# Expert outputs of a mixture of experts put on their tokens by matmuls, in place of scatters to memory and loads

## The reference

```python
def hier_moe(h, ...):
    g_prob = softmax(h @ w_rg + b_rg);  p_top, g_top = top_k(g_prob, 1)
    e_in_group = (h @ w_re + b_re).reshape(n, 4, 8)[arange(n), g_top[:, 0]]
    v_top, i_top = top_k(e_in_group, 2)
    gates = softmax(v_top) * p_top                # two experts of 32 for each token
    ...                                           # tokens sorted by expert, in blocks
    out = (silu(xb @ w_gate[e]) * (xb @ w_up[e])) @ w_down[e]     # each block xb
    y = segment_sum(out * w_buf[:, None], tok_buf)                # gated, summed on the tokens
# after it: x = x + y, then the final RMSNorm
```

## Time and profile before

| | |
|---|---|
| median of 3 runs | 1119.4 us (1118.56 to 1120.49) |
| profiled execution, its own time | 1122.52 us |
| its span | 1120.7 us |
| mean granted clock of TensorE | 0.962 |
| DMA busy share from about 625 us on | 1.0, at about 427 GB/s |

### The profile page before, as it was taken

The page is one execution under the profiler, slowest core; times in us unless marked ns, Lnnn a source line. Parts: engine busy times, 40 slices in busy tenths (PEclk is TensorE's granted clock), DMA queues, the critical chain, the costliest instruction groups (busy, mean ns, idle before and its releaser), DMA issues.

```text
span 1120.7 us, 15303 instructions
## 1 busy us (share of the span) xinstructions
PE 1025.1 (91%) x6339; PEld 701.9 (63%) x6339; DVE 380.1 (34%) x727; ACT 281.6 (25%) x454; POOL 223.6 (20%) x129
## 2 busy tenths in 40 slices
PE   8999999999999999999999899977888889877886
PEld 6996777779999879999998333333333333333332
DVE  7246332233587491421344322111011111111117
ACT  5435434346446442222213100000000000000003
POOL 0331112112312256434330011110011110110000
PEclk9999999999999989999999999999888999998898
DMA  9332411212211213253285999999999999999993
GB/s 225 81 88 79 164 50 39 57 39 74 60 48 39 67 57 91 80 164 100 80 351 224 346 427 426 426 425 427 427 427 427 427 428 427 428 427 425 426 410 136
DMA packets 108943, 267.57 MB, mean 239 GB/s; under 512 B 21821, under 2 KB 88797, under 8 KB 95666
## 3 DMA queue, kind: packets, MB, share of 16 engines
q1 hardware_dynamic: 104178, 258.06, 60.0%
q0 software_dynamic: 4704, 8.64, 2.0%
HBM read 256.12 MB, written 18.17 MB: 245 GB/s over the span
## 4 chain that ended last, share of the span: by engine, by line
PE 37%; DMA 24%; DVE 4%; issue 2%; ACT 2%; POOL 1%; SPq 0%; DVEq 0%; ACTq 0%; POOLq 0%
DMA we<-in_w_exp_up 24%; PE proj L1051 16%; PE proj L1533 12%; PE proj L1549 3%; DVE ors L2089 1%; PE bank L1425 1%; DVE xsT L2536 1%; PE bank L1559 1%; PE proj L1331 0%; ACT ex L1873 0%; PE proj L1535 0%; DVE gqk L2361 0%; POOL wlo L905 0%; PE bank L1027 0%; PE bank L1626 0%
## 5 line engine op out<-in xcount | busy, mean ns | idle before, releaser
L1533 PE MATMUL proj<-we,xsT 128*64 128x512 f32 x512 | 252.1, 650 | 66.4 <-DMA we<-in_w_exp_up 58.6
L1535 PE MATMUL proj<-we,xsT 128*64 128x512 f32 x512 | 252.5, 651 | 0.0
L905 POOL TENSOR_TENSOR wlo<-raw,whi 128x1024 fp32r<-128x1024 f32 x68 | 155.7, 2290 | 397.9 <-PE proj L1051 373.4
L1533 PEld LDWEIGHTS proj<-we,xsT 128*64 128x64 f32 x512 | 73.6, 150 | 212.2 <-issue 198.1
L1051 PE MATMUL proj<-hT_hi,whi 128*128 128x272 f32 x688 | 147.7, 296 | 2.0 <-DVEq L2313 2.0
L1051 PE MATMUL proj<-hT_hi,wlo 128*128 128x272 f32 x688 | 145.3, 293 | 0.0
L1051 PE MATMUL proj<-hT_lo,whi 128*128 128x272 f32 x688 | 145.3, 293 | 0.0
L2528 DVE TENSOR_TENSOR hg<-hg,proj 64x512 f32<-64x512 f32 x32 | 22.1, 690 | 310.2 <-ACT hg L2043 293.9
L2043 ACT ACTIVATE hg<-proj 64x512 f32<-64x512 f32 x30 | 17.7, 590 | 422.0 <-PE proj L1535 422.0
L1549 PE MATMUL proj<-we,hT 128*64 128x512 f32 x256 | 115.2, 593 | 1.1 <-DVE hT L2531 1.1
L1550 PE MATMUL proj<-we,hT 128*64 128x512 f32 x256 | 115.2, 592 | 0.0
(11 more groups left out here) (364 smaller groups left out, 1430.9 us busy)
## 6 DMA issues: line engine op xcount, KB each, us to landing
we<-in_w_exp_gate SPq DMA_DIRECT2D x31, 2048.0 KB, 32.0
we<-in_w_exp_up SPq DMA_DIRECT2D x31, 2048.0 KB, 36.6
we<-in_w_exp_down SPq DMA_DIRECT2D x31, 2048.0 KB, 39.0
raw<-in_w_in SPq DMA_DIRECT2D x43, 512.0 KB, 3.8
x_rows<-in_x_prompt SPq DMA_DIRECT2D x8, 512.0 KB, 5.2
raw<-in_w_branch_b SPq DMA_DIRECT2D x8, 512.0 KB, 3.9
raw<-in_w_out SPq DMA_DIRECT2D x8, 512.0 KB, 4.0
zc<-expert_out SPq DMA_DIRECT2D x4, 1024.0 KB, 16.7
```

Of the source, the lines that this page charges most:

```text
L905: nc.gpsimd.tensor_tensor(lo[:, 0:c], raw[n % NRAW][:, 0:c], hi[:, 0:c].bitcast(F32), ALU.subtract).then_inc(w_split, 1)
L1533: pe.matmul(proj[0:SLOTS, s, 0, :], xsT[:, k, cols], wg[:, k * FF:(k + 1) * FF], start=(k == 0), stop=(k == KD - 1))
L1535: mm = pe.matmul(proj[64:64 + SLOTS, s, 0, :], xsT[:, k, cols], wu[:, k * FF:(k + 1) * FF], start=(k == 0), stop=(k == KD - 1))
```

## The change

Nothing is scattered to memory or loaded back. The gate of each slot is brought to its lane once, as `slot_gates`, by 40 small matmuls of the slot map (`on_lanes`), and `gated` multiplies by it, so that an expert's output rows are weighted already. When down(u) is done, ScalarE copies the output rows to `yo_hi` in fp32r (two instructions of 64x512, `rows_high`), and VectorE subtracts that from the PSUM rows and writes the rest to `yo_lo` (two of 64x512, `rows_low`). The two experts of a pair lie on lanes 0 to 63 and 64 to 127.

For each pair VectorE makes `pair_pick` (128x544, fp32r), which is 1 where a slot's token number is the column's. Then, while the next pair's second expert runs, TensorE puts the pair's rows on the tokens, one tile of tokens after the other: four fp32r matmuls for each (two halves of 512 columns, high and low), into banks 0 and 1. These stand before k-steps 3, 5 and 7 of up, and before k-steps 0 and 2 of down. VectorE adds each tile to X (`add_tile`), and the next tile's matmuls wait for that, since there is one place for them in PSUM; `turn_rows` waits for all five. The tiles of the 15th pair stand in the tail (`rows_ahead`), each ahead of `last_rows` of the same tile, and the first inside up(30). `last_rows` has picks of ones. `add_gated`, `second_rows`, the zeroing of `expert_out` (4.25 MB early on), the scatters and the loads of `zc` are gone, and so is the copy of the gates to rows (L1523).

```diff
...
+UP_PICKS = (3, 5, 7)
+DOWN_PICKS = (0, 2)
...
-    ys = nc.dram_tensor("expert_out", (4 * TOK, FF), F32, kind="Internal").ap()
...
@@ sync
-        sp.wait_ge(all_stored, 1)
-        pair_rows = ys.rearrange("(t x) d -> t (x d)", x=4)
-        for i in range(NT):
-            sp.dma_start(zc[i][0:ROWS[i], :, :]...pair_rows[i * P:i * P + ROWS[i], :]).then_inc(rows_loaded[i], 16)
...
@@ gpsimd
         def pair(it, m):
-            if not first_pair(it, m):
-                put(it, 2 * m - 1)
-            put(it, 2 * m)
             if not last_pair(it, m):
                 pool.wait_ge(gidx_ready, it * NSETS + m + 3)
...
@@ tensor
         pe.wait_ge(last_gates_ready, 1)
-        for s in range(2):
-            row = proj[:, s, :, :].rearrange("p a b -> p (a b)")
-            for i in range(NT):
-                ...
-                mm = pe.transpose(row[:, i * P:i * P + r], last_gates[...]...)
+        on_lanes(bank[:, 3, 0:NBLK], 0, token_at, True, False)
+        on_lanes(bank[:, 3, 0:NBLK], 1, token_at, False, True).then_inc(second_done, 1)
...
+        def tile_rows(i, lanes_, done, at=0):
+            r = ROWS[i]
+            for half in range(2):
+                pe.matmul(bank[0:r, at + half, :], pair_pick[lanes_, i * P:i * P + r], yo_hi[lanes_, half, :], start=True, stop=False)
+                mm = pe.matmul(bank[0:r, at + half, :], pair_pick[lanes_, i * P:i * P + r], yo_lo[lanes_, half, :],
+                               start=False, stop=True)
+            mm.then_inc(done, 1)
+
+        def pair_rows(it, m, i):
+            if i:
+                pe.wait_ge(rows_added, it * (NT * NSETS) + NT * (m - 1) + i)
+            else:
+                pe.wait_ge(yo_ready, it * (2 * NSETS) + 2 * m)
+            tile_rows(i, slice(0, P), rows_picked)
 
         def pair(it, m):
...
-                up(s, slice(s * SLOTS, (s + 1) * SLOTS), w[0], w[1], up_done)
-                if u or not first_pair(it, m):
-                    go_down(it, u - 1)
+                up(s, slice(s * SLOTS, (s + 1) * SLOTS), w[0], w[1], up_done, in_up if s and beside else None)
+                if u or beside:
+                    go_down(it, u - 1, in_down if s and beside else None)
                 if s:
+                    if beside:
+                        pe.wait_ge(rows_added, it * (NT * NSETS) + NT * m)
                     turn_rows(it * (16 * NSETS) + 16 * m + 32)
...
-        last_rows(0, 1, True, False)
+        rows_ahead(1)
+        last_rows(0, 1, False, False)
         pe.wait_ge(last_y, 2)
         last_rows(1, 0, False, True)
-        second_rows(1, False)
         last_rows(1, 1, False, True)
         for i in range(2, 4):
-            last_rows(0, i, True, False)
-            second_rows(i, False)
+            rows_ahead(i)
+            last_rows(0, i, False, False)
             last_rows(1, i, False, True)
         pe.wait_ge(comb_done, 1)
-        last_rows(0, 4, True, False)
+        rows_ahead(4)
+        last_rows(0, 4, False, False)
         last_rows(1, 4, False, True)
...
@@ scalar
+        def expert_high(s, lane, done):
+            for half in range(2):
+                last = nc.scalar.copy(yo_hi[lane, half, :], proj[half * SLOTS:(half + 1) * SLOTS, s, 1, :])
+            last.then_inc(done, 1)
...
@@ vector
-            v.tensor_tensor(hg[0:SLOTS, s, :], hg[0:SLOTS, s, :], proj[64:64 + SLOTS, s, 0, :], ALU.mult).then_inc(done, 1)
+            v.scalar_tensor_tensor(hg[0:SLOTS, s, :], hg[0:SLOTS, s, :], slot_gates[0:SLOTS, cols], proj[64:64 + SLOTS, s, 0, :],
+                                   ALU.mult, ALU.mult).then_inc(done, 1)
...
+        def expert_low(s, lane, done):
+            for half in range(2):
+                last = v.tensor_tensor(yo_lo[lane, half, :], proj[half * SLOTS:(half + 1) * SLOTS, s, 1, :],
+                                       yo_hi[lane, half, :].bitcast(F32), ALU.subtract)
+            last.then_inc(done, 1)
...
+        def make_picks(q):
+            cols = bass.ds(q, 1) if not isinstance(q, int) else slice(q, q + 1)
+            v.tensor_scalar(pair_pick[:, :], numbers, pair_tokens[:, cols], None, ALU.is_equal)
+
+        def add_tile(i, done, at=0):
+            r = ROWS[i]
+            xi = X[0:r, i, :].rearrange("p (a b) -> p a b", a=2)
+            v.tensor_tensor(xi, xi, bank[0:r, at:at + 2, :], ALU.add).then_inc(done, 1)
...
-        add_gated(0, 0)
-        step.settle()
-        add_gated(0, 1)
-        add_gated(1, 0)
         for i in range(NT):
             add_last(i)
-            if i + 2 < NT:
-                add_gated(i + 2, 0)
...
```

More of the change, by code:

```diff
@@ L74 @@
                   ("iota32", NE), ("over_base", NE), ("round", NE), ("blocks", NOVER), ("neg_lane", SLOTS), ("iota_blk", NBLK),
-                  ("token", NT), ("half", 1)):
+                  ("token", NT)):
     CONST_AT[_name] = (_c, _n)
@@ L691, in _build @@
     U_ = Region(RT)
-    pick = [U_(f"pick{s}", [P, TOK]) for s in range(2)]
-    xsb2 = U_("xsb2", [P, D])
+    pair_pick = U_("pair_pick", [P, TOK], F32R)
+    yo_lo = U_("yo_lo", [P, 2, FF], F32R)
+    pick = [U_("pick0", [P, TOK]), nc.alloc_sbuf_tensor_at("pick1", [P, TOK], F32, offset=G_FIN + D * 4)]
     assert U_.at <= LAST
+    xsb2 = nc.alloc_sbuf_tensor_at("xsb2", [P, D], F32, offset=G_FIN + D * 4)
+    assert G_FIN + 2 * D * 4 <= W_G2 + GH * DK * 4
     numbers = con("rope")
-    second = nc.alloc_sbuf_tensor_at("second", [P, 3, P], F32, offset=W_G2)
     def pick_out(i):
@@ L1530, in up @@
             for k in range(KD):
-                if half and k in (0, KD // 2):
+                if half:
                     half(k)
@@ L1546, in down @@
             for k in range(4):
-                if half and k in (0, 2):
+                if half:
                     half(k)
@@ L1591, in _ @@
         with pe.If(n_more > 0):
-            pe.wait_ge(yo_ready, NE - 2)
+            for i in range(NT):
+                pair_rows(ROUNDS, 0, i)
+            pe.wait_ge(rows_added, NT * (PAIRS - 1))
             with pe.Fori(0, NOVER) as b:
@@ L2484, in _ @@
         dve.wait_ge(maps_done, 1)
-        token, choice = bank[:, 2, 0:NBLK], bank[:, 3, 0:NBLK]
+        token = bank[:, 2, 0:NBLK]
         for s in range(2):
@@ L2505, in _ @@
         run(v.tensor_tensor(gate[:, 1, :], gate[:, 0, :], rd, ALU.mult))
-        run(v.tensor_tensor(both_gates, O[:, :, :, NE - 2:NE], gate[:, :, :].unsqueeze(3).to_broadcast([P, 2, NT, 2]), ALU.mult))
-        v.tensor_tensor(last_gates[:, :, :], both_gates[:, 0], both_gates[:, 1], ALU.add).then_inc(last_gates_ready, 1)
+        for c in range(2):
+            last = v.tensor_tensor(token_at[:, c], is_blk[:, c], across(gate, c, NBLK), ALU.mult)
+        last.then_inc(last_gates_ready, 1)
+        for s in range(2):
+            lane = slice(s * SLOTS, (s + 1) * SLOTS)
+            step(v.tensor_copy(pair_tokens[lane, :], G1[lane, 0:NE].rearrange("p (q s) -> p q s", s=2)[:, :, s]))
         run(v.tensor_tensor(nbe, starts[0:1, 1:NE + 1].unsqueeze(1).to_broadcast([1, NOVER, NE]),
@@ L2514, in _, with gated @@
         v.tensor_copy(meta[0:1, :], bef[0:1, :]).then_inc(meta_ready, 1)
-        run(v.tensor_scalar(S1[:, :], G1[:, :], 4.0, con("half"), ALU.mult, ALU.add))
         dve.wait_ge(second_done, 1)
-        run(v.scalar_tensor_tensor(S1[:, :], choice, 2.0, S1[:, :], ALU.mult, ALU.add))
+        run(v.tensor_copy(slot_gates[:, :], bank[:, 3, 0:NBLK]))
         dve.wait_ge(meta_ready, 1)
         dve.wait_ge(late_loaded, 32)
-        for s in range(2):
-            dve.wait_ge(gate_rows_done, s + 1)
-            row_ = proj[:, s, :, :].rearrange("p a b -> p (a b)")[:, 0:TOK]
-            last = v.scalar_tensor_tensor(pick[s][:, :], numbers, G1[:, NE - 2 + s:NE - 1 + s], row_, ALU.is_equal, ALU.mult)
-        last.then_inc(picks_ready, 1)
-        def gated(s, done):
-            v.tensor_tensor(hg[0:SLOTS, s, :], hg[0:SLOTS, s, :], proj[64:64 + SLOTS, s, 0, :], ALU.mult).then_inc(done, 1)
+        dve.wait_ge(x2_copied, NT)
+        def gated(s, e, done):
+            cols = bass.ds(e, 1) if not isinstance(e, int) else slice(e, e + 1)
+            v.scalar_tensor_tensor(hg[0:SLOTS, s, :], hg[0:SLOTS, s, :], slot_gates[0:SLOTS, cols], proj[64:64 + SLOTS, s, 0, :],
+                                   ALU.mult, ALU.mult).then_inc(done, 1)
         def hidden_copy(s, done):
@@ L2572, in _ @@
         with dve.If(n_more > 0):
-            for s in range(2):
-                dve.wait_ge(ys_stored[s], 16 * (PAIRS - 1))
+            for i in range(NT):
+                pair_rows(ROUNDS, 0, i)
             dve.wait_ge(xs_loaded, 16 * PAIRS)
```

186 lines of the change are left out of this document (92 added, 94 removed).

## The result

| | before | after |
|---|---|---|
| median of the timed runs, us | 1119.95 (1118.56 to 1121.39, 4 runs) | 1133.5 (1131.56 to 1135.21, 4 runs) |
| ratio, 95% interval | | 1.0118 (1.0101 to 1.0135) |
| profiled execution, own time / span, us | 1122.52 / 1120.7 | 1131.56 / 1129.7 |
| predicted, us | | 1128.3 (1114 to 1139) |

The change costs 13.5 us by the medians. Run again beside fresh runs of the kernel before, it took 1134.42 us against 1120.43, a ratio of 1.0122 (1.0100 to 1.0144).

What follows compares the result with a forecast made beforehand. The weights' DMA was taken to bound the kernel before, TensorE after, at 30.5 us a pair. Loop +11.3, up(30)'s weight wait -0.3 and tail -2.1 made +8.9 us on 1119.4: 1128.3 us, range 1114 to 1139.

Steps and rivals of the forecast that it cites:

- The forecast's case: In the loop, TensorE's 30.5 us a pair sets the end, giving 1128.3 us; chance 0.67.
- What bounds it: Loop over pairs: the weights' DMA sets the pace before; afterwards TensorE does, as the DMA starts 21 us ahead.
- the tile: Four fp32r matmuls on TensorE, 0.90 us, plus 0.30 going in and out: 1.20 us, five a pair 6.0.
- The wait: Before the fourth tile, TensorE waits for VectorE's add of the third: 0.4 us a pair, bounds 0.2 and 0.6.
- The waits costed at nothing: First tile's wait for `yo_low`, and those for `gated`, `turn_rows` and `make_picks`: hidden behind other work, 0 us.
- The tail: From the last down's end VectorE needs 18.2 us instead of 21.5; with up(30)'s first tile at +1.2, -2.1 us.
- What the DMA gets back: Queue 0 without scatters: 0.7 us a pair, making the DMA pace 30.55 us instead of 31.23.
- The signs: In the profile: `xsT` every 30 to 31 us, clock 1.00, no weight waits, DMA under 1.0, tail 3 us shorter.
- The zeroing: Early on, 4.25 MB where queues were two to three tenths busy: removing it was given no gain.
- Cheap changes: At each tile's entry and exit, tiling changes cost 0.19 us: 29.7 us a pair, 1117.1 us; chance 0.15.
- TensorE under the DMA's pace: In the loop, picks nearly hidden: TensorE needs 28.6 us a pair, weights decide, 1107.8 us; chance 0.06.
- A second wait: First tile comes 1.5 us late through slower copies or low halves: 32 us a pair, 1149 us; chance 0.12.

Runs made afterwards that it cites:

- the second: Second profiled execution of the changed kernel, nothing altered: span 1133.3 us.
- the twins: Changed kernel plus five tiny matmuls a pair between up's k-steps: at full width (layout changes) 1155.71 us, on their neighbours' 64-lane layout 1139.33 us.
- the three groups: Changed kernel with two PSUM places for the tiles, put in three groups between k-steps instead of five: 1117.6 us, ratio 0.9975.
- three with two beside transposes: Changed kernel reordered: two tiles within up, next rows' transposes and one tile, down, two tiles, hidden rows' transposes; other PSUM places: 1111.32 us, ratio 0.9913.

## Why the prediction was right, and where its terms were off

The forecast's case came true: TensorE became the bound, by picks, changes of layout and one wait a pair. The measured 1133.5 us is 5.2 us above the predicted 1128.3.

- **What bounds it.** Right. The table of waits has no DMA, and without the tiles the weights stop the loop at 1053.3; I had 1055.
- **The mis-sized term is the tile.** Predicted 0.90 + 0.30 = 1.20 us; it is 0.93 + 0.34 = 1.27. The matmul of 512 columns takes 0.233 us, not 0.225. Of its 0.125 us for 272 columns I held 0.011 fixed, and the bound in which all of it grows with the columns (0.94 a tile) was nearer. For going in and out I counted the entry and the exit in rows where one side was a transpose or a half-height matmul; here there are four parts: 0.10 ahead, 0.10 in the first matmul, 0.09 behind, 0.05 in the next step. The prediction had no term of its own for the one in the first matmul. Five tiles are 6.27 us instead of 6.0. The pair is 30.78 instead of 30.5; over the loop it is +15.1 instead of +11.3.
- **The wait.** Right: 0.37 in the trace and 0.39 by taking it away; I had 0.4. It sat before the fourth tile, as forecast.
- **The waits costed at nothing.** Right. VectorE had the last low half of a pair ready at 753.7 and the first tile started at 754.32: the margin is 0.6 us; I had 0.5. The make_picks row took 0.50 us, the estimate was 0.73.
- **The tail.** 18.4 us from the end of down, I had 18.2. With the wait of up(30) it is -2.4 as forecast (4.1 in the profiled pair less the 1.7 of the clock).
- **What the DMA gets back.** 1.1 us a pair instead of 0.7, without effect, since TensorE decides.
- **The signs.** `xsT` every 30 to 31 us, no wait for weights, one wait a pair and the shorter tail came as named. Two signs did not: the DMA share stayed at 1.00 to 1.01 where it was to fall under 1.0, and the clock was not at 1.00 throughout in each execution (0.93 from 600 to 650 us in the second). Neither touches the bound.
- **The zeroing.** It lay at 91 to 135 us, where the earlier trace rows shows two and four tenths, not two and three. Taking it away brought the first `xsT` forward by no more than executions differ anyway.
- **Why the sum looked exact.** The profiled pair differ by 9.0 us and I had 8.9, but that is chance: a loop 3.8 us longer than forecast, and 3.6 us (1.9 and 1.7) by which the two single executions happened to differ. Of the 5.2 us by which the median was missed, 3.8 are the loop; 0.6 is the median of before, which stood at 1119.95 in these runs instead of 1119.4; the other 0.8 is within the spread of the runs. That the profiled execution took 1131.56 us, and 1131.4 was forecast for it, is the same chance.
- **The rivals.** Cheap changes: refuted by the twins and by the three groups. TensorE under the DMA's pace: not in this kernel, but it is what halving the matmuls or reordering brings, at 1111 us. A second wait: there was none.

## What to carry to other kernels

This change put 6.6 us of TensorE time into some 7 us of waits and lower clock a pair, and lost: over the 14 pairs the kernel before took only 29.7 us each, since its first ones ran at 24.1 on weights that lay ready. So compare each candidate bound over the whole loop, head start included, and not pair by pair. Here extra matmuls in a loop of half-width ones were best put in few groups, and beside work that already has their layout: five groups and a wait cost 13.5 us here, three groups without the wait nothing (1117.6 us), and three with two beside transposes won 9. A reordering that is worthless under one bound (the kernel before: 1.0004) can be worth something once the bound has moved (there it took 0.67 us off a pair while TensorE led), so try it again after each change.

## What the runs showed of the hardware that was not expected

Going from two half-width outputs to full width and back costs on both sides of both borders: 0.34 us around four fp32r matmuls of 512 columns, and 0.26 for one bf16 matmul of 4 columns, against 0.06 for the same tiny matmul in its neighbours' layout. Behind a change the weight load starts with its matmul and no longer a step ahead. In the tiles 0.10 of the 0.34 stands in the first matmul (0.03 with 32 columns of weights), and this part stays behind transposes of the same width. And short stretches at the lower clock come at places that differ between executions of one program, about 1.7 us each where one could be singled out (a first pair of 23.93 us instead of 22.24, a tail of 53.8 instead of 52.1). Two single executions differed by 3.6 us outside what the change did, more than a quarter of it.
